# Moving the next block's row transposes into the middle of a weight piece in a mixture-of-experts loop

## The reference, cut to what matters

```
def _moe(h, router_w, router_b, w_gate, b_gate, w_up, b_up, w_down, b_down):
    ...
    xb = h[buf_tok].reshape(n_blocks, MOE_BLOCK, h.shape[-1])

    def expert_block(args):
        xe, e = args
        gate = jnp.minimum(xe @ w_gate[e] + b_gate[e], SWIGLU_LIMIT)
        up = jnp.clip(xe @ w_up[e] + b_up[e], -SWIGLU_LIMIT, SWIGLU_LIMIT)
        act = (up + 1) * (gate * jax.nn.sigmoid(SWIGLU_ALPHA * gate))
        return act @ w_down[e] + b_down[e]
    ...
```

## Time and profile before

| what | value |
|---|---|
| median of 3 runs | 2912.07 us (2909.96 to 2912.74) |
| the profiled execution: time / span | 2911.7 us / 2909.9 us |
| PE busy over the span | 2847.5 us, 98% |
| DVE, ACT, POOL busy | 69%, 55%, 19% |
| DMA, mean rate | 220 GB/s |
| in the expert loop, 2000 to 2100 us: PE, DVE, ACT, POOL busy of 100 us | 100.00, 92.05, 76.28, 28.09 |

### The profile page before, as it was taken

How to read it: one execution, slowest core, us unless ns; L and a number is a source line. 1 busy time by engine, 2 the same in 40 slices (tenths; PEclk the granted TensorE clock), 3 DMA queues, 4 the chain that set the end, 5 groups by cost and what they waited for, 6 DMA issues and landing times.

```text
span 2909.9 us, 41501 instructions
## 1 busy us (share of the span) xinstructions
PE 2847.5 (98%) x15068; PEld 2301.5 (79%) x15068; DVE 2021.8 (69%) x2243; ACT 1612.0 (55%) x1758; POOL 546.6 (19%) x479
## 2 busy tenths in 40 slices
PE   8999999998999999999999899999999999999999
PEld 4788888765788888877788688888888888888887
DVE  8742234587622326847743799999999999999998
ACT  5332323346522324445632677777777777777775
POOL 1012100113012000003100222222222222232221
PEclk9999999998999999999999999999999999999999
DMA  8422221220122322110022899999999999999995
GB/s 348 184 81 107 102 99 75 91 87 32 56 104 87 125 92 95 58 59 16 1 92 89 314 404 386 386 386 386 385 386 384 382 385 384 383 384 381 382 385 218
DMA packets 88925, 638.89 MB, mean 220 GB/s; under 512 B 10449, under 2 KB 11665, under 8 KB 26097
## 3 DMA queue, kind: packets, MB, share of 16 engines
q1 hardware_dynamic: 78592, 599.97, 52.8%
q0 software_dynamic: 9936, 36.75, 4.7%
q10 hardware_dynamic: 288, 0.65, 0.1%
HBM read 611.28 MB, written 26.05 MB: 219 GB/s over the span
## 4 chain that ended last, share of the span: by engine, by line
PE 53%; DVE 1%; ACT 0%; issue 0%; SPq 0%; DMA 0%; POOL 0%; ACTq 0%; DVEq 0%
PE banks L263 15%; PE banks L265 15%; PE banks L264 15%; PE banks L3411 1%; PE banks L3271 1%; PE banks L3393 1%; PE banks L2338 1%; PE banks L2205 1%; PE banks L2234 1%; PE banks L2361 1%; PE banks L2217 1%; DVE arena_rounded L3290 1%; PE banks L2349 0%; PE banks L3377 0%; DMA arena_rounded<-bias_dram 0%
## 5 line engine op out<-in xcount | busy, mean ns | idle before, releaser
L3290 DVE TENSOR_TENSOR arena_rounded<-arena,arena_rounded 128x2048 fp32r<-128x2048 f32 x420 | 951.0, 2286 | 89.0 <-ACT arena_rounded L3286 89.0
L3286 ACT ACTIVATE arena_rounded<-arena 128x2048 fp32r<-128x2048 f32 x420 | 801.6, 1918 | 207.5 <-PE banks L265 132.8
L263 PE MATMUL banks<-arena_rounded,operand_rounded 128*128 128x512 f32 (+1 forms) x2064 | 817.2, 396 | 2.7 <-DVE small_rounded L3582 1.3
L264 PE MATMUL banks<-arena_rounded,operand_rounded 128*128 128x512 f32 (+1 forms) x2064 | 801.6, 388 | 0.0
L265 PE MATMUL banks<-arena_rounded,operand_rounded 128*128 128x512 f32 (+1 forms) x1504 | 583.1, 388 | 0.0
L263 PEld LDWEIGHTS banks<-arena_rounded,operand_rounded 128*128 128x128 f32 x2064 | 387.8, 188 | 82.5 <-issue 2.9
L264 PEld LDWEIGHTS banks<-arena_rounded,operand_rounded 128*128 128x128 f32 x2064 | 388.2, 188 | 76.7 <-issue 1.0
L265 PEld LDWEIGHTS banks<-arena_rounded,operand_rounded 128*128 128x128 f32 x1504 | 282.4, 188 | 58.8
L263 PE MATMUL banks<-operand_rounded,arena_rounded 128*128 128x512 f32 (+1 forms) x728 | 272.9, 375 | 0.1
L265 PE MATMUL banks<-operand_rounded,arena_rounded 128*128 128x512 f32 (+1 forms) x728 | 270.5, 372 | 0.0
L264 PE MATMUL banks<-operand_rounded,arena_rounded 128*128 128x512 f32 (+1 forms) x728 | 270.3, 371 | 0.0
(11 more groups left out here) (525 smaller groups left out, 3856.6 us busy)
## 6 DMA issues: line engine op xcount, KB each, us to landing
arena<-in_gate SPq DMA_DIRECT2D x140, 1024.0 KB, 7.7
arena<-in_up SPq DMA_DIRECT2D x140, 1024.0 KB, 7.8
arena<-in_down SPq DMA_DIRECT2D x140, 1024.0 KB, 6.0
arena<-in_dense SPq DMA_DIRECT2D x62, 2048.0 KB, 7.8
arena<-in_dense SPq DMA_DIRECT2D x6, 1024.0 KB, 4.9
small<-in_rows SPq DMA_DIRECT2D x7, 512.0 KB, 8.0
resid<-in_x SPq DMA_DIRECT2D x4, 512.0 KB, 8.3
expert_sums<-operand SPq DMA_DIRECT2D x4, 512.0 KB, 4.4
```

Of the source, the lines that this page charges most:

```text
L263: nc.tensor.matmul(out, left[0], right[0], start=start, stop=False)
L264: nc.tensor.matmul(out, left[0], right[1], start=False, stop=False)
L3286: nc.scalar.activation(high[q % NHI], raw[:, q, :], ACT.Copy).then_inc(high_ready, 1)
L3290: nc.vector.tensor_tensor(low[q], raw[:, q, :], high[q % NHI].bitcast(F32), ALU.subtract).then_inc(low_ready, 1)
```

## The change

`down_products` gets an argument `next_rows`. Where it is true, as in all turns of the loop, the wait for `x_in` and the eight row transposes stand right behind the four transposes of inner group 1, ahead of the last six products of piece 9. The last block, which has no next block, passes False. No instruction is added or taken away inside a turn.

```
-            def down_products(b, q):
+            def down_products(b, q, next_rows=True):
                 down_waits(b, q)
                 for j in range(2):
                     for c in range(2):
                         i = down_product(q, j, c)
                     if q == 9 and j == 0:
                         turn_hidden(b, 1)
+                        if next_rows:
+                            pe.wait_ge(x_in, 16 * b + 32)
+                            turn_rows()
                 return i
...
                             for q in range(8, PIECES):
                                 down_products(b, q).then_inc(used, 1)
-                                if q == 9:
-                                    pe.wait_ge(x_in, 16 * b + 32)
-                                    turn_rows()
...
             for q in (8, 9):
-                down_products(last, q).then_inc(used, 1)
+                down_products(last, q, next_rows=False).then_inc(used, 1)
```

## The result

The changed kernel takes 2929.34 us, the median of 6 runs (2923.99 to 2935.89), against 2911.48 (2909.96 to 2914.88, 6 runs) before. The ratio is 1.0059, 95% interval 1.0049 to 1.0069: slower, as forecast, but outside the range of 2917 to 2927.

The account below looks back on a forecast made before the run. PE was taken to set the loop's pace without a hole. 33 new holes of 0.36 us made 11.9, less 0.3 saved by the transposes, 11.6 us: 2923 us, or 0.38% slower, range 2917 to 2927.

Parts of the forecast that it names:

- What bounds the kernel: Expert loop: PE's own work fills the 35.485 us block period, so any hole in PE is paid in full.
- The transposes together: PE, piece 9: twelve transposes in a row save between nothing and 0.03 us per turn, 0.01 taken.
- The chain: Piece 9's count, 0.875 us late, passes through ACT and DVE; the rows' low part reaches PE 0.475 later.
- The DRAIN you can't avoid: Skill rule for DVE: no next operation until the pipeline is empty; would make the hole 0.44, sum 2.6 us more.
- the margins: Lateness swallowed on the way to PE's next block: 0.40 us at DVE and 0.11 at PE.
- The hole: PE standing still at each block start in the loop: 0.36 us, bounds 0.28 to 0.44.
- the sum: Whole kernel: 33 x 0.36 = 11.9, less 0.3 for the transposes, is 11.6 us on the profiled 2911.7.
- How it would look: Signs in the changed profile: period some 35.83 us, about 0.59 instead of 0.23 between products at the block start.
- The wait for the rows, POOL, SP, piece 10: Other waits the move touches: 10 us remain for the rows, POOL unchanged, SP's load hidden, piece 10 free but narrow.
- slower still: Rival: piece 10 also waits 0.1 to 0.2 us for the inner group's low part, 2926 to 2930 us; 8 in 100.
- How the numbers follow: Chances and range: forecast 2919 to 2926 at 80 in 100; range 2917 to 2927 with bounds and run spread.

Follow-up runs that it names:

- e4: Kernel before with three more transposes of a constant behind the row transposes, into a bank nobody reads; 2924.44 us, ratio 1.0040.
- e2_rows_first: Changed kernel with the rows' high part (ACT) and low part (DVE) ahead of those of the next block's piece 1; 2911.1 us, ratio 0.9992.
- e7_wait_at_third: Changed kernel, a block's first two products wait for the rows' high part only, the low part's wait stands at the third; 2913.51 us, ratio 1.0000.
- e3: Kernel before, PE untouched, ACT's wait for the row transposes moved ahead of the next block's piece 1 high part; 2928.39 us, ratio 1.0056.
- e5: Changed kernel with four of the eight row transposes moved ahead, the other four behind piece 9's last product; 2912.44 us, ratio 1.0001.
- e6: Changed kernel with six of the eight row transposes moved ahead, two behind piece 9's last product; 2919.29 us, ratio 1.0019.

## Why the prediction was right in its mechanism and wrong in its time

- **What bounds the kernel**: right. PE's pace in the loop is the loop's pace; a hole (changed kernel) and extra work of the same length (e4) both cost their full 34-fold.
- **The transposes together**: forecast 0.01 us saved per turn, between nothing and 0.03. e2_rows_first and e7_wait_at_third, which have them together and no hole, run at 35.455 and 35.467 against 35.485: 0.02 to 0.03, the upper end of it.
- **The chain**: right link by link. ACT's wait forecast 1.59, measured 1.58; DVE's low part of piece 1 forecast 0.475 later, measured 0.46 (as idle time, forecast about 0.45, the row shows 0.38); load behind DVE 0.13 forecast and measured. DVE's rows overlap as the prediction let them: the rows' low part starts at 2011.70, 0.09 ahead of the recorded end of piece 1's (2009.50 + 2.29 = 2011.79). The section of the Trainium skill that the prediction weighs against this (VectorE: DVE Perf Modes, "The DRAIN you can't avoid") says itself that a next operation which is not held starts earlier, so the rows do not speak against it. e2 and e7 take the chain apart at two places and the loss goes; e3 makes it without the move and the loss comes; e5 and e6 confirm the margins it has to eat through.
- **The hole**: forecast 0.36, measured 0.36 in the two PE steps. But the block's start costs some 0.40 in all, taken against the period of e2, whose program for PE is the same (35.861 - 35.455): about 0.03 more lies in the six steps behind the hole, 2013.38 to 2014.77 or 1.39 us, as in e5. The prediction had no term for that. Half of the excess is given back by the transposes, which save more than forecast. The period to be seen was given as 35.83 and is 35.86; over the loop that makes 12.4 us where the sum had 11.6, short by 0.8.
- **How it would look**: I wrote a distance of 0.59 between the two products. It is 0.50, and the remaining 0.09 stand in the next step: a product behind a pause is recorded early, with its load. As a length of hole it was right, as a reading it was not.
- **The wait for the rows, POOL, SP, piece 10**: free, as forecast. The rival "slower still" didn't occur: PE goes on from piece 9's last product to piece 10's first in 0.24 us. POOL still stands at the block's output until 2015.23, with 12.36 us of waiting (12.39 before). PE, then POOL:

```profile
2007.11 0.39 PE L265 MATMUL banks<-arena_rounded,small_rounded 128*128 128x512 f32 x1
2007.35 0.39 PE L263 MATMUL banks<-arena_rounded,operand_rounded 128*128 128x512 f32 x1
```

```profile
2015.23 1.59 POOL L3353 DMA_INDIRECT expert_sums<-operand,arena  x1 [12.36 <-ACT operand L3541]
```

- **The step that failed** is the one in "How the numbers follow" that said the range "takes in the forecast with its bounds and the spread of the runs (2909.96 to 2912.74)". Three runs of the kernel before stood for the spread of all. They happened to hold none of the upper group, some 10 us above the rest, to which 3 of 15 and 9 of 33 later runs of the same kernel belong; of the changed kernel's first six runs three did, which was chance as far as these runs tell. So a term of some 10 us that the sum and the range put at nothing is what carried the measured median out of the range; the 0.8 us by which the hole was short would not have. The median of the six, 2929.34, is the mean of one run of either group (2925.53 and 2933.15). The lower group alone, 2924.0 to 2925.5, is inside the range. The later ratios, 1.0047 and 1.0041, measured against 15 and 33 runs of the kernel before, are nearer to the forecast 1.0038 than the first, 1.0059, whose interval (from 1.0049) doesn't reach it. A share of the upper group that differs between the two kernels is not shown: 7 of 21 runs of the changed kernel against 12 of 54 of the one before, and one run of either kernel (2929.1 and 2918.6) lies between its groups, the first counted as upper and the second not.

No version beats both kernels by more than can be measured: e2_rows_first, with a ratio of 0.9992 (0.9981 to 1.0003), keeps the 0.03 us per turn that the transposes together save, which is 1.0 us over the loop.

## What to carry to other kernels

A step moved forward on the engine that sets the pace is paid for by whatever it is moved ahead of: list the counts that now come later, and follow each through the other engines' hand-written orders back to the pacing engine, with the margin of each link. Where the moved step's own result is wanted early, the order of the engines that use it has to move as well; here that alone turned 12 us of loss in the loop into none. A margin that is used up to its end is not quite free either: in e5 it cost 0.02 us per turn without a hole. And three runs of a kernel are too few to know its spread: a range needs a term for what the stages outside the change do from run to run.

## What the runs showed of the hardware that was not expected

From 100 to 121 us PE ran at a granted clock of 0.96 in one execution of the same program and of 0.51 in another, with 556 and 276 matmuls recorded, and the first block start of the loop came 10 us later. PE was busy for all of that stretch in both (21.00 of 21 us), so busy time doesn't tell the two apart; the mean granted clock of the whole execution (0.992 and 0.990) barely does.
